# Hyena: the direct term as a tap of the filter in PSUM, and another order of outputs, filter products and the prompt's steps

## The reference

```python
def _hyena_filters(L, lp):
    ...                                   # hdn: three sine layers over positions, L x 64
    filt = (hdn @ lp['f_w3']).reshape(L, HYENA_ORDER, 2, D_MODEL)
    window = jnp.exp(-t * deltas[None])   # t = linspace(0, 1, L); 1 at t = 0
    return filt * window[:, None, None, :]

def _bidir_long_conv(u, h_fwd, h_bwd, bias):
    L = u.shape[1]
    kern = jnp.concatenate([h_fwd, 0, h_bwd[:0:-1]], axis=0)
    y = irfft(rfft(u, n=2 * L) * rfft(kern))[:, :L]
    return y + u * bias

u = x1 * _bidir_long_conv(v, filt[:, 0, 0], filt[:, 0, 1], bias[0])
u = x2 * _bidir_long_conv(u, filt[:, 1, 0], filt[:, 1, 1], bias[1])
```

## Time and profile before

| | before |
|---|---|
| median of 3 runs | 4986.24 us (4981.21 to 4990.27) |
| profiled execution | 4986.92 us, span 4985.1 us |
| mean granted clock of TensorE | 0.953 |
| busy share of the span | TensorE 92%, VectorE 49%, ScalarE 19% |
| Hyena stage, 3225.78 to 3848.50 us | 622.72 us; TensorE 530.65 us busy, VectorE 485.05 us, clock 0.92 |

### The profile page before, as it was taken

How to read it: one execution, slowest core, us unless ns; L and a number is a source line. 1 busy time by engine, 2 the same in 40 slices (tenths; PEclk the granted TensorE clock), 3 DMA queues, 4 the chain that set the end, 5 groups by cost and what they waited for, 6 DMA issues and landing times. The chain is left out here.

```text
span 4985.1 us, 72919 instructions
## 1 busy us (share of the span) xinstructions
PE 4602.1 (92%) x31522; PEld 3433.5 (69%) x31522; DVE 2459.4 (49%) x3771; ACT 932.0 (19%) x1628; POOL 453.1 (9%) x360
## 2 busy tenths in 40 slices
PE   5999799978999999999999999888987999999997
PEld 4775366647999756777756577677766577777554
DVE  6672688855666414222225366568777342222002
ACT  2010255542222202111100021111110121111001
POOL 1120100000000001212100022100000021221000
PEclk6999799978999899999999999999998999999998
DMA  5241000031100021111144232200101211112110
GB/s 183 85 146 54 15 1 1 1 130 45 25 21 21 13 101 51 43 34 43 34 142 142 81 104 85 92 24 32 43 21 65 81 37 34 43 36 77 40 35 38
DMA packets 303146, 286.47 MB, mean 57 GB/s; under 512 B 57632, under 2 KB 258697, under 8 KB 302506
## 3 DMA queue, kind: packets, MB, share of 16 engines
q1 hardware_dynamic: 273386, 191.61, 12.7%
q0 software_dynamic: 11280, 44.04, 2.5%
q10 hardware_dynamic: 18160, 46.15, 2.5%
HBM read 223.18 MB, written 58.59 MB: 57 GB/s over the span
## 5 line engine op out<-in xcount | busy, mean ns | idle before, releaser
L544 PE MATMUL acc<-arena 128*128 128x288 f32 x7504 | 1834.2, 407 | 23.1 <-ACT arena L599 11.2
L544 PEld LDWEIGHTS acc<-arena 128*128 128x128 f32 x7504 | 1427.8, 191 | 427.7 <-issue 12.3
L671 PE MATMUL acc<-arena 128*128 128x384 f32 x2880 | 940.5, 489 | 13.3 <-PEq L126 8.0
L671 PEld LDWEIGHTS acc<-arena 128*128 128x128 f32 x2880 | 549.6, 191 | 396.7 <-issue 22.7
L804 DVE TENSOR_TENSOR arena<-acc,arena 128x576 f32<-128x576 f32 x44 | 33.3, 758 | 846.4 <-PE acc L544 846.4
L731 DVE SCALAR_TENSOR_TENSOR arena<-acc,arena 128x128 f32<-128x128 f32 (+1 forms) x96 | 47.6, 516 | 630.2 <-PE acc L671 630.2
L599 ACT ACTIVATE arena<-acc 128x576 f32<-128x576 f32 x201 | 130.6, 650 | 1077.1 <-PE acc L544 1077.1
L297 DVE SCALAR_TENSOR_TENSOR arena<-arena 128x512 f32<-128x512 f32 x336 | 245.1, 770 | 13.5 <-issue 0.9
L1167 PE MATMUL acc<-arena 128*128 128x128 f32 x1296 | 203.3, 297 | 42.3 <-DVE arena L1282 39.0
L711 ACT ACTIVATE arena<-arena 128x384 f32<-128x384 f32 x96 | 50.2, 523 | 970.4 <-DVE arena L731 810.1
L1167 PEld LDWEIGHTS acc<-arena 128*128 128x128 f32 x1296 | 165.9, 197 | 88.2 <-issue 83.3
(11 more groups left out here) (310 smaller groups left out, 5289.3 us busy)
## 6 DMA issues: line engine op xcount, KB each, us to landing
arena<-in_ffn_w SPq DMA_DIRECT2D x88, 512.0 KB, 5.1
arena<-in_ada_w ACTq DMA_DIRECT2D x12, 2048.0 KB, 12.4
arena<-in_ada_w POOLq DMA_DIRECT2D x24, 1024.0 KB, 5.6
arena<-in_ffn_w SPq DMA_DIRECT2D x14, 1408.0 KB, 7.0
arena<-scratch_x_d ACTq DMA_DIRECT2D x32, 576.0 KB, 9.4
scratch_z_d<-arena SPq DMA_DIRECT2D x28, 576.0 KB, 2.8
arena<-scratch_z_d SPq DMA_DIRECT2D x28, 576.0 KB, 4.9
scratch_x_d<-arena POOLq DMA_DIRECT2D x24, 576.0 KB, 4.1
```

The source lines that it names most:

```text
L544: last = pe.matmul(self.k.bank(bank + h, QC), left[:, q, :], right[:, q, h * QC:(h + 1) * QC], start=(q == 0 and p not in self.ON_TOP), st ...
L671: last = pe.matmul(k.bank(3 * (m % 2) + tc, TC), weight(m, kt), src(kt)[:, cols(tc)], start=(kt == 0), stop=(kt == n_k - 1))
```

## The change

The bias leaves the parameter table. It is loaded for each step as one row of 256 values (`hb`), with one more DMA behind the three that load `w3`. TensorE adds it to the filter: after the product for the tile that holds time 0 (in `make_filter`, and in the prompt's "filt") a product of one row with row 0 of the identity, 256 columns wide, accumulates the bias on the tap of time 0 of the forward filter. The window is 1 there. `out_latent` and `out_prompt` are then one multiplication each, from PSUM by the gate.

The order is another one. On TensorE, p = 2 and 3 of `make_filter` move behind the next step's spectrum hi, "freq" behind spectrum lo, "inv" behind the whole filter spectrum of f = 0 (its result moves from bank 4 to bank 0), "tok" between the two halves of the inverse, "filt" between its residues 3 and 0. On VectorE the prompt's window stands ahead of the outputs, the prompt's product between `spectrum_1` and `spectrum_2`, and `out_prompt` behind `product`. ScalarE's copies follow: its last two windows stand behind the copies of the turned u, "freq" is copied right behind the spectrum's first part.

```diff
+    hb = [k.at(CST + CCOL["blockones"][0] + Q * o, Q)[0:1, :] for o in range(2)]
...
+                sp.dma_start(hb[o], A["hy_bias"][0, o:o + 1, c]).then_inc(w3_in[o], 16)
...
+            def direct_tap(m, at):
+                return pe.matmul(at[:, 0:Q], k.ident[0:1, :], hb[m % 2], start=False, stop=True, skip_group_check=True)
...
+                    if t == 0:
+                        direct_tap(m, bank(4))
...
@@ tensor, the loop over n @@
                     spectrum(n, 0, "hi")
+                if ok(n + 1):
+                    pe.wait_ge(dve_w.sem, dve_w.at(n + 1, "w0"))
+                    make_filter(n + 1, 2)
+                    pe.wait_ge(dve_w.sem, dve_w.at(n + 1, "w1"))
+                    make_filter(n + 1, 3)
+                if ok(n):
+                    pe.wait_ge(act_t.sem, act_t.at(n, "b1"))
+                    spectrum(n, 0, "lo")
                     pe.wait_ge(act_p.sem, act_p.at(n, "tok"))
...
-                    pe.wait_ge(act_t.sem, act_t.at(n, "b1"))
-                    spectrum(n, 0, "lo")
...
                     if ok(n):
                         pe.wait_ge(act_u.sem, act_u.at(n, "c0"))
-                        pe.wait_ge(dve_p.sem, dve_p.at(n, "out"))
                     filter_spectrum(n + 1, 0, "hi")
+                    if ok(n):
+                        pe.wait_ge(dve_p.sem, dve_p.at(n, "prod"))
                     filter_spectrum(n + 1, 0, "lo")
...
                     spectrum(n, 1, "hi")
-                    pe.wait_ge(dve_u.sem, dve_u.at(n, "lo0"))
+                    pe.wait_ge(dve_p.sem, dve_p.at(n, "out"))
                     spectrum(n, 1, "lo")
...
                     pe.wait_ge(dve_u.sem, dve_u.at(n, "ab1"))
-                    for b in ORDER:
+                    for b in ORDER[0:2]:
+                        inverse(n, 1, b).then_inc(pe_i.sem, 1)
...
+                    direct_tap(n + 1, bank(4)).then_inc(pe_p.sem, 1)
+                if ok(n):
+                    for b in ORDER[2:4]:
                         inverse(n, 1, b).then_inc(pe_i.sem, 1)
                 if ok(n + 2):
                     pe.wait_ge(w3_set, n + 3)
...
                     make_filter(n + 2, 0)
                     make_filter(n + 2, 1)
-                    pe.wait_ge(dve_w.sem, dve_w.at(n + 2, "w0"))
-                    make_filter(n + 2, 2)
-                    pe.wait_ge(dve_w.sem, dve_w.at(n + 2, "w1"))
-                    make_filter(n + 2, 3)
...
@@ vector @@
             def out_latent(n, b):
...
-                dve.drain()
-                for m in range(QT):
-                    dve.scalar_tensor_tensor(out=tb[:, m * Q:(m + 1) * Q], in0=u[:, m, times(b)], scalar=k.col("hbias", 8 * o + i * QT + m),
-                                             in1=bank(b)[:, m * Q:(m + 1) * Q], op0=ALU.mult, op1=ALU.add)
-                dve.drain()
-                tt(u[:, :, times(b)], pair(tb[:, 0:512]), gate[o][:, :, times(b)], ALU.mult).then_inc(dve_e.sem, 1)
+                tt(u[:, :, times(b)], pair(bank(b)), gate[n % 2][:, :, times(b)], ALU.mult).then_inc(dve_e.sem, 1)
...
                 if ok(n):
                     spectrum_1(n, 0)
-                    dve.wait_ge(g_in[o], 16 * QT * (i + 1))
-                    out_prompt(n)
+                    prompt_product(n)
                     spectrum_2(n, 0)
                     product(n, 0)
+                    out_prompt(n)
                     spread(n, 0)
...
                     filter_spectrum(n + 1, 1)
+                    prompt_window(n + 1)
                 if ok(n):
                     for b in ORDER:
                         out_latent(n, b)
```

More of the change, by code:

```diff
@@ L2350, in _ @@
                         pe.wait_ge(act_u.sem, act_u.at(n, "c0"))
[L2351 removed]
                     filter_spectrum(n + 1, 0, "hi")
+                    if ok(n):
+                        pe.wait_ge(dve_p.sem, dve_p.at(n, "prod"))
                     filter_spectrum(n + 1, 0, "lo")
                 if ok(n):
+                    pe.wait_ge(dve_u.sem, dve_u.at(n, "lo0"))
+                    pe.wait_ge(dve_p.sem, dve_p.at(n, "prod"))
+                    for m in range(QT):
+                        for c in range(2):
+                            last = pe.matmul(bank(0)[:, m * 128:(m + 1) * 128], pa[:, c * Q + m * 128:c * Q + (m + 1) * 128], ptab[:, 2 + c, :],
+                                             start=(c == 0), stop=(c == 1))
+                    last.then_inc(pe_p.sem, 1)
                     if ok(n + 1):
@@ L2376, in _ @@
                         inverse(n, 0, b)
+                if ok(n + 1):
+                    u = u_of(n + 1)
+                    pe.wait_ge(v_in[((n + 1) // 2) % 2], 16 * QT * ((n + 1) // 4 + 1))
+                    pe.wait_ge(act_f.sem, act_f.at(n + 1, "c1"))
+                    for m in range(QT):
+                        last = pe.transpose(bank(4)[:, m * 128:(m + 1) * 128], u[:, m, 0:NP_], k.ident)
+                    last.then_inc(pe_p.sem, 1)
                 if ok(n):
                     pe.wait_ge(dve_u.sem, dve_u.at(n, "ab1"))
-                    for b in ORDER:
+                    for b in ORDER[0:2]:
+                        inverse(n, 1, b).then_inc(pe_i.sem, 1)
+                if ok(n + 1):
+                    pe.wait_ge(act_p.sem, act_p.at(n + 1, "tok"))
+                    pe.matmul(bank(4), hd[:, 0:NP_], w3[(n + 1) % 2].rearrange("p e n -> p (e n)"), start=True, stop=False, skip_group_check=True)
+                    direct_tap(n + 1, bank(4)).then_inc(pe_p.sem, 1)
+                if ok(n):
+                    for b in ORDER[2:4]:
                         inverse(n, 1, b).then_inc(pe_i.sem, 1)
@@ L2573, in _ @@
                 if ok(n + 2):
-                    window(n + 2, 0)
-                    window(n + 2, 1)
-                    window(n + 2, 2)
-                    window(n + 2, 3)
-                if ok(n + 1):
-                    dve.wait_ge(pe_p.sem, pe_p.at(n + 1, "filt"))
-                    dve.wait_ge(act_p.sem, act_p.at(n + 1, "win"))
-                    tt(pair(psd), pair(bank(5)), twice(pw), ALU.mult).then_inc(dve_p.sem, 1)
-                    dve.wait_ge(pe_p.sem, pe_p.at(n + 1, "freq"))
-                    dve.wait_ge(act_p.sem, act_p.at(n + 1, "freq"))
-                    tt(pair(yb[:, 0:512]), pair(bank(6)), twice(pk[:, 0:Q]), ALU.mult)
-                    tt(pair(yb[:, 512:1024]), pair(bank(6))[:, 1::-1, :], twice(pk[:, Q:512]), ALU.mult)
-                    dve.drain()
-                    tt(pa[:, 0:Q], yb[:, 0:Q], yb[:, 512:768], ALU.subtract)
-                    tt(pa[:, Q:512], yb[:, Q:512], yb[:, 768:1024], ALU.add).then_inc(dve_p.sem, 1)
+                    for p in range(4):
+                        window(n + 2, p)
 def stage_hyena_out(k, A, scratch, x_stored, out_in):
```

76 lines of the change are left out of this document (32 added, 44 removed).

## The result

| | before | changed kernel |
|---|---|---|
| first series | 4986.41 us (4981.21 to 4990.27, 4 runs) | 4957.45 us (4953.90 to 4960.52, 4 runs): ratio 0.9943 [0.9928, 0.9958] |
| second series, another time | 4984.75 us (4980.56 to 4992.60, 9 runs) | 4951.26 us (4949.31 to 4959.22, 5 runs): ratio 0.9932 [0.9920, 0.9944] |
| profiled execution | 4986.92 us, span 4985.1 us | 4960.52 us, span 4958.7 us |
| mean granted clock | 0.953 | 0.959 |
| Hyena stage | 622.74 us | 591.95 us |

The forecast was 4950 us, with a range of 4932 to 4967 us.

What follows compares the result with a forecast made beforehand. TensorE (92% of the span) was taken as the bound, VectorE as second. Six steps 30.6, step 6 to step 7 3.0 and the end 2.8 sum to 36.4 us off 4986.9: 4950 us, range 4932 to 4967.

Steps and rivals of the forecast that it cites:

- VectorE's chain and the gap: VectorE from s (start of "freq") to the second `spread`'s end: s + 41.9 us; TensorE then waits 4.3 us every step.
- From the gap to the next s: TensorE behind the new gap until the next "freq" starts: 24.5 us of work, plus 2.5 us for the clock.
- The tap: Bias product on TensorE in `make_filter` and "filt": 0.43 us each, bounds 0 and 0.9; wrong if above 0.5.
- The outputs: VectorE's outputs, now one multiplication each: 1.07 us, bounds 0.69 and 1.76, hidden behind TensorE's work.
- The clock behind the gap: TensorE's inverse behind the new gap: lower clock costs 2.5 us; under 0.8 for some us, 1.00 elsewhere.
- the rival in which it holds: Products behind the new gap run in full clock, 2.5 us less in each of seven steps: 4932 us; chance 0.12.
- the one in which it lasts twice as long: Behind the gap the clock stays low twice as long: another 2.5 us a step, 4967 us; chance 0.13.
- The start: Stage's start: added DMA 0.6 us and three taps 1.3 us against the 2.73 us gap going: 0, within 2.
- Step 6 to step 7: Last step, no filter products, TensorE waits for shorter outputs: 3.0 us off 56.5, bounds 0 and 5.1.
- The end: VectorE's last output behind the last inverse: 4.1 us becomes 1.3 with one multiplication, 2.8 us less.
- the 2.73 us gap: TensorE's wait for `out_prompt` ahead of the filter spectrum in nearly every step; claimed to go, nothing taking its place there.
- the 5.56 us gap: TensorE's wait ahead of `make_filter` p = 2 for window 0, which stands behind four `out_latent` on VectorE; claimed to go.

Runs made afterwards that it cites:

- The tap alone: Against the kernel before: bias added by TensorE, outputs of one multiplication, old order kept; 4929.40 us, ratio 0.9893, and 4932.30 us when run again.
- the order alone: Against the changed kernel: bias added by VectorE in the old form, no tap, new order kept; 4982.35 us, ratio 0.9996 to the kernel before.
- e5_mixed_order: Changed kernel with `make_filter` p = 2, 3, "freq" and the prompt's product moved back, and "filt" put into the gap; 4930.01 us.
- e6_mixed_filled: e5_mixed_order plus four products nobody reads, ahead of "filt" in what is left of the gap; 4925.95 us.
- e3_fill_gap: Changed kernel plus seven products of 256 columns nobody reads, ahead of TensorE's wait for the second `spread`; 4939.64 us.

## Why the prediction was right, and where it was not

- **VectorE's chain and the gap.** The chain ends at s + 41.85 (41.9 forecast), TensorE comes there with 4.31 us to spare (4.3 forecast), in every step. In the middle steps `out_prompt` finds "inv" done, and `make_filter` its windows. This part of the working holds to 0.1 us.
- **From the gap to the next s** took 3434.64 − 3407.71 = 26.9 us in the step shown, 27.2 on average (69.06 − 41.85); 24.5 (its terms add up to 24.6) and 2.5 of clock were forecast. The sum is right by luck, by two errors that cancel: the filled gap shows the clock's price as 1.9 us, so the work is 25.3. Half of the 0.8 us is the tap.
- **The tap** takes 0.63 us from its start to the next product's (3413.80 to 3414.43), not 0.43. It is above the 0.5 that the prediction named as the point where it would be wrong on this; two of them a step cost 0.4 us more than taken. In the trace the load of its weights starts together with it (3413.80), and the next product's with that product (3414.43), where elsewhere the load runs 0.21 us ahead (3412.64 for the product at 3412.85); that fits the 0.2 us.
- **The outputs** take 4.12 / 4 = 1.03 us each one behind the other (1.07 forecast; 1.05 to 1.09 singly in the last step). The Trainium skill's remark on cachelines (SBUF — State Buffer, Door 1) is borne out so far: 512 elements with steps of four in the gate and in the output take 1.03, those without such steps 0.69, both with an operand from PSUM.
- **The clock behind the gap** fell in each step, to 0.79 over 8 us in the step shown, and was back at 1.00 after that; over the 16 records behind the gap alone it was 0.53 to 0.71 in steps 0 to 6. In most steps 16 records took 5.1 to 5.4 us, in two of seven 6.7. So the rival in which it holds is out, the one in which it lasts twice as long came in part in two steps, and TensorE came back each time. The loop whose wait throws the clock back in every pass, of which the Trainium skill tells (TensorE: Matmul & The Clock Gate, HAM oscillation), is what the trace has here, in those seven steps, with a wait for VectorE in place of one for a DMA; filling the wait ended it.
- **The start** (0 ± 2 forecast, +3.0 measured) is a term that was mis-sized, beyond its bounds. Its three taps take 2.9 us, not 1.3, as two of them run at the lower clock:

```profile
3238.92 1.22 PE L2313 MATMUL acc<-arena 1*128 1x256 f32 x2
3240.07 8.07 PE L2319 MATMUL acc<-arena 128*128 128x512 f32 x14
...
3276.25 2.06 PE L2319 MATMUL acc<-arena 128*128 128x512 f32 x2 [3.36 <-DVE arena L2552]
3278.24 1.22 PE L2313 MATMUL acc<-arena 1*128 1x256 f32 x2
3279.39 5.46 PE L2319 MATMUL acc<-arena 128*128 128x512 f32 x6
```

  The filter products wait 3.36 us for the prompt's window (2.61 before, for the filter's spectrum). The tap alone reaches its first inverse 3.3 us later too (95.57 us), the order alone 2.5 us earlier (89.78). Between the order alone and the changed kernel lie 5.5 us. Two taps of 1.15 us are 2.3 of them (the third stands ahead of the 3.36 us wait, which is 3.98 without it). The filter products beside the two taps take 3.2 us longer, because TensorE stays longer at the lower clock (granted 0.59 from 3276.25 to 3286.60, and 0.76 over the same work in the order alone): 16 of their records 1.2 us and 8 of them 1.9 us, 7.3 instead of the 5.3 in the order alone:

```profile
3265.26 5.49 PE L2315 MATMUL acc<-arena 128*128 128x512 f32 x8 [3.98 <-DVE arena L2551]
```

  The added DMA of the earlier trace rows delays nothing: the wait for GpSimd at the start is 17.7 us, before 17.9.
- **Step 6 to step 7** (−3.0 forecast, −1.7 measured). The prediction checked the waits for "inv" and `out_prompt` in a middle step, where a whole filter spectrum, 10.4 us, covers them. The last step has none, and TensorE waits 3.00 and 3.57 us there. But VectorE sets the time in it, and runs on from 3773.96 to 3793.40 without a pause; it waits only 0.54 us, for spectrum lo of f = 1:

```profile
3753.15 6.65 PE L2327 MATMUL acc<-arena 128*128 128x256 f32 x16 [4.31 <-DVE arena L2522]
...
3793.94 1.23 DVE L2493 TENSOR_TENSOR arena<-acc,arena 128x1024 f32<-128x1024 f32 x1 [0.54 <-PE acc L2299]
```

  So the two waits cost 0.5 us. The tap alone takes 7.4 us off this part (56.52 to 49.15), more than the upper bound of 5.1. The order puts 5.7 back on: 2.7 from half to half of step 6's inverse (3741.55 to 3753.15, 11.60 us against 8.87), 2.6 on VectorE from its first butterfly to the last step's inverse (2.2 of it the prompt's product in the chain, 0.5 that wait), and 0.3 between them.
- **The end** (−2.8 forecast) gave −2.5.
- **What the prediction left out** is a price for each half. Its sentence that the 2.73 us gap goes "and nothing takes its place there" holds for that place, but it does not ask what that gap is worth. Each gap of the kernel before had its own cause. The short outputs alone remove the 5.56 us gap and the clock's loss behind it; with them VectorE's chain sets the time, so the other gap, 2.05 us by then, costs nothing. The order makes this chain 2.2 us longer (41.85 against 39.7). In return it takes "freq" and "tok", 1.9 us, out of TensorE's work behind the second `spread`; but its gap of 4.31 us costs 1.9 us of clock, and that stretch stays at 27.2 us (27.3 in the tap alone). This is the 2.1 us by which a step of the changed kernel is longer than one of the tap alone. The prediction had the 2.2 us of the prompt's product in its chain, and the new gap, but never set them against what the order brings. The forecast of the whole was right; a forecast for the tap alone would have shown that the order is not worth having.

What is not settled: why the lower clock lasts longer at the start with the taps, and why the stages ahead of Hyena vary by up to 10 us from one execution to another.

## What to carry to other kernels

When a change has two halves, price each on its own and then both: here one half brought 7.0 us a step, the other 1.4, and both together 5.0. Moving a step into the time in which TensorE is busy is no gain where the engine that does it is the late one; look whose idle time the step had filled before. Check every wait also in the last pass of the loop, where the work that covers it is missing, and ask there too which engine sets the time: 6.6 us of TensorE's waits cost 0.5 us here, since VectorE ran on.

## What was not expected of the hardware

- Short gaps already lower the clock, and not every time: behind gaps of 1.67 to 1.70 us in `e5_mixed_order`, each with a wait of 0.47 us shortly ahead of it, the same 32 records took 7.17 us in four steps, 8.86 in two and 10.22 in one:

```profile
3595.15 7.17 PE L2327 MATMUL acc<-arena 128*128 128x256 f32 x32 [1.67 <-DVE arena L2517]
...
3660.25 8.86 PE L2327 MATMUL acc<-arena 128*128 128x256 f32 x32 [1.67 <-DVE arena L2517]
...
3727.05 10.22 PE L2327 MATMUL acc<-arena 128*128 128x256 f32 x32 [1.69 <-DVE arena L2517]
```

  Behind 0.47 us, which comes in every step of `e6_mixed_filled`, the middle steps show no fall.
- A product of one row cost no less than one of 128: 0.63 us for 256 columns here, against 0.43 for each of the two in "freq".
- A series of products that nobody needs can make a kernel faster: 1.9 us a step in `e3_fill_gap`, 0.6 in `e6_mixed_filled`.
